# Gate and up of the four FFNs as seven block products over feature pairs, input halves and token halves

## The reference

```python
def rms_norm(x, g):
    y = x * lax.rsqrt(jnp.mean(x * x, axis=-1, keepdims=True) + RMS_EPS)
    return y * g
def swiglu(x, w_gate, w_up, w_down):
    return (jax.nn.silu(x @ w_gate) * (x @ w_up)) @ w_down
for layer in range(DEPTH):
    x = x + 0.5 * swiglu(rms_norm(x, ffn_norm1[layer]), ...)   # ffn0, ffn2
    h = rms_norm(x, mix_norm[layer])
    x = x + mixer(h)                      # mla_mixer, or swa with shared k, v
    x = x + 0.5 * swiglu(rms_norm(x, ffn_norm2[layer]), ...)   # ffn1, ffn3
    if layer == 0:
        kv = rms_norm(x, kv_norm) @ w_kv_shared
y = rms_norm(x, final_norm)
```

## Time and profile before

| | |
|---|---|
| median of 3 runs | 2532.2 us (2528.36 to 2532.36) |
| profiled execution | 2525.54 us, its span 2523.7 us |
| TensorE busy | 2455.3 us (97%), 16448 matmuls |
| VectorE, ScalarE, GpSimd busy | 46%, 30%, 35% |
| granted TensorE clock | 0.995 of full speed |
| HBM traffic | 83 GB/s over the span |

### The profile page before, as it was taken

One profiled execution on the slowest core, in us unless ns is written; L12 is line 12 of the kernel. 1 busy time (PEld: TensorE's weight loads), 2 busy tenths in 40 slices (PEclk: granted clock), 3 DMA queues, 4 the chain that ended last, 5 costly groups with the idle time before them and its releaser, 6 DMA issues.

```text
span 2523.7 us, 42391 instructions
## 1 busy us (share of the span) xinstructions
PE 2455.3 (97%) x16448; PEld 2340.2 (93%) x16448; DVE 1155.6 (46%) x2378; ACT 767.8 (30%) x1505; POOL 881.4 (35%) x592
## 2 busy tenths in 40 slices
PE   8999999998999999999999999999999999999997
PEld 8999999987666999999999999999986899999997
DVE  6434343665355453434346434343455464343435
ACT  6121222423255332121215222222246432222223
POOL 2333333443123334242424433333245243333332
PEclk9999999999999999999999999999999999999998
DMA  5222223234242122222222321212123122222211
GB/s 171 76 75 75 75 75 91 94 137 158 80 149 82 59 76 83 67 79 70 77 73 76 93 91 58 91 58 90 52 105 104 40 93 76 75 75 75 75 50 42
DMA packets 72607, 210.80 MB, mean 84 GB/s; under 512 B 7681, under 2 KB 22049, under 8 KB 71745
## 3 DMA queue, kind: packets, MB, share of 16 engines
q1 hardware_dynamic: 72512, 209.55, 26.3%
HBM read 191.22 MB, written 18.30 MB: 83 GB/s over the span
## 4 chain that ended last, share of the span: by engine, by line
PE 88%; DVE 4%; issue 2%; ACT 2%; POOL 1%; SPq 1%; DMA 1%; DVEq 0%; ACTq 0%; POOLq 0%
PE psa L356 17%; PE psa L357 17%; PE psa L358 17%; PE psb L356 10%; PE psb L357 10%; PE psb L358 10%; DVE split L479 1%; PE psb L1032 1%; PE psa L1168 1%; PE psa L1001 1%; PE psb L1187 1%; DVE work L404 1%; PE psb L1175 1%; PE psa L1002 1%; POOL wa L343 1%
## 5 line engine op out<-in xcount | busy, mean ns | idle before, releaser
L356 PE MATMUL psa<-split,wa 128*128 128x320 f32 (+1 forms) x3040 | 944.5, 311 | 24.4 <-DVE split L479 16.8
L358 PE MATMUL psa<-split,wa 128*128 128x320 f32 x3024 | 935.8, 309 | 0.0
L357 PE MATMUL psa<-split,wa 128*128 128x320 f32 x3024 | 935.7, 309 | 0.0
L343 POOL TENSOR_TENSOR wb<-raw,wb 128x1024 fp32r<-128x1024 f32 (+1 forms) x99 | 235.4, 2378 | 1205.6 <-ACT wb L335 1178.4
L356 PEld LDWEIGHTS psa<-split,wa 128*128 128x128 f32 x3040 | 573.9, 189 | 28.5 <-DVE wa L461 9.6
L357 PEld LDWEIGHTS psa<-split,wa 128*128 128x128 f32 x3024 | 570.8, 189 | 0.9 <-issue 0.2
L358 PEld LDWEIGHTS psa<-split,wa 128*128 128x128 f32 x3024 | 570.5, 189 | 0.0
L343 POOL TENSOR_TENSOR wa<-raw,wa 128x1024 fp32r<-128x1024 f32 x205 | 490.4, 2412 | 169.8 <-ACT wa L335 169.8
L356 PE MATMUL psb<-acts,wb 128*128 128x320 f32 x1440 | 447.4, 311 | 1.9 <-DVE xs L687 1.7
L687 DVE SCALAR_TENSOR_TENSOR xs<-psb,xs 128x320 f32<-128x320 f32 x720 | 341.3, 488 | 229.6 <-PE psb L358 229.6
L357 PE MATMUL psb<-acts,wb 128*128 128x320 f32 x1440 | 444.7, 309 | 0.0
(11 more groups left out here) (222 smaller groups left out, 2169.7 us busy)
## 6 DMA issues: line engine op xcount, KB each, us to landing
raw<-in_w SPq DMA_DIRECT2D x310, 512.0 KB, 3.9
park<-xs SPq DMA_DIRECT2D x2, 2560.0 KB, 9.0
work<-in_c_latT SPq DMA_DIRECT2D x8, 512.0 KB, 3.9
work<-in_c_lat SPq DMA_DIRECT2D x8, 512.0 KB, 3.6
xs<-park SPq DMA_DIRECT2D x1, 2560.0 KB, 14.5
xs<-park SPq DMA_DIRECT2D x2, 1280.0 KB, 5.5
y_out<-xs SPq DMA_DIRECT2D x8, 320.0 KB, 3.4
work<-v_park SPq DMA_DIRECT2D x8, 256.0 KB, 3.0
```

Of the source, the lines that this page charges most:

```text
L343: nc.gpsimd.tensor_tensor(lo[:, 0:n], raw[:, (p % RAW_SLOTS) * PIECE:(p % RAW_SLOTS) * PIECE + n], hi[:, 0:n].bitcast(F32), ALU.subtract). ...
L356: nc.tensor.matmul(ps, w[0], xx[1], start=first, stop=False)
L357: nc.tensor.matmul(ps, w[1], xx[0], start=False, stop=False)
L358: return nc.tensor.matmul(ps, w[0], xx[0], start=False, stop=last)
```

## The change

Two neighbouring feature tiles, the two halves of the 8 input tiles and the two token halves make a 2 x 2 by 2 x 2 block product, done with seven products in place of eight, for gate and for up. Of a pair's weights, VectorE forms the sums s1, s2, s3 and s4 in `raw` (`sum_first`, `sum_second`, `sum_fourth`), each operand of 128 x 512 is copied by ScalarE (`operand_hi`) and split by GpSimd (`operand_lo`) into a ring of 7 slots; there are 14 operands a pair (7 kinds, gate and up). The activations are now scaled with gain and `rstd` ahead of the first product (`x_first` for b11 and b21, `x_second` for t1, b22, t2, n4, t3), summed and split into seven parts that stay in place for the whole FFN; three of them lie in buffers of other phases, so the keys and values are stored and read back ahead of the window phase. Running sums in PSUM are copied out by ScalarE between products (`act_snap`), and VectorE adds a snapshot and a bank for three of the four (tile, half) results (`dve_combine`). Silu, product and its split are as before, and so are the down products, their order and their evictions. The transitions into the FFNs are rewritten: FFN1's squares and sums, which VectorE and ScalarE made ahead of it, are now made during the output projection, and the first weight sums and splits stand there too. The table of the window's biases is read behind FFN2.

The diff, cut to the loops of an FFN:

```diff
+KINDS = ("a11", "a12", "s1", "s2", "s3", "a22", "s4")
+X_OF = {"a11": "b11", "a12": "b21", "s1": "t1", "s2": "t2", "s3": "t3", "a22": "n4", "s4": "b22"}
+OPS = 2 * len(KINDS)
+GU = OPS * PAIRS
+SNAPS, SUMS, COMBS, PRODS = 6 * PAIRS, 8 * PAIRS, 3 * PAIRS, 4 * PAIRS
+RING, RING_AT = 7, 4
+QUARTER = DT // 2
+HALVES = {"a11": (0, 0), "a12": (0, 1), "s2": (0, 0), "s1": (1, 0), "a22": (1, 1), "s4": (0, 1)}
+SUM_TURN = {"s3": 0, "s1": 1, "s2": 4, "s4": 6}
+REGION = [dict(zip(("b11", "b21", "b22", "t2", "t1", "t3", "n4"), range(7)))] * 4
+REGION[2] = dict(zip(("n4", "b11", "b21", "b22", "t2", "t1", "t3"), range(7)))
...
+            place = ffn_place(p - RAW_SLOTS)
+            if place and place[2] < 4:
+                i, pair, n = place
+                sp.wait_ge(s_lo, at(it, 28, GU * i + OPS * pair + 13 + n // 2))
+            else:
+                sp.wait_ge(w_lo, at(it, 4, N_SINGLE[p - RAW_SLOTS + 1]))
...
+    def operand_hi(act, i, it, pair, j):
+        kind, m, n = KINDS[j // 2], j % 2, OPS * pair + j
+        if kind in ("a11", "a12", "a22"):
+            wait_landed(act, i, pair, m, HALVES[kind][0], it)
+        else:
+            act.wait_ge(s_sum, at(it, 16, SUMS * i + 8 * pair + SUM_TURN[kind] + (m if kind in ("s2", "s4") else 2 * m) + 1))
+        if n >= RING:
+            act.wait_ge(gu_mm, at(it, 28, GU * i + n - RING + 1))
+        elif i:
+            act.wait_ge(*RING_BEFORE[i][0 if (j + RING_AT) % RING >= 4 else 1])
+        nc.scalar.activation(ring_hi[:, (j + RING_AT) % RING, :], operand(i, pair, kind, m), ACT.Copy).then_inc(s_hi, 1)
...
+    def operand_lo(pool, i, it, pair, j):
+        r = (j + RING_AT) % RING
+        pool.wait_ge(s_hi, at(it, 28, GU * i + OPS * pair + j + 1))
+        nc.gpsimd.tensor_tensor(ring_lo[:, r, :], operand(i, pair, KINDS[j // 2], j % 2), ring_hi[:, r, :].bitcast(F32),
+                                ALU.subtract).then_inc(s_lo, 1)
...
+    def sum_first(dve, i, it, pair, m, kind):
+        if kind == "s3":
+            for f in range(2):
+                wait_landed(dve, i, pair, m, f, it)
+            if pair:
+                dve.wait_ge(s_lo, at(it, 28, GU * i + OPS * (pair - 1) + 8 + m + 1))
+            elif i:
+                dve.wait_ge(*RING_BEFORE[i][0])
+            nc.vector.tensor_tensor(s3_of[m], raw_half(i, pair, m, 0, 0), raw_half(i, pair, m, 1, 0), ALU.subtract).then_inc(s_sum, 1)
+        else:
+            nc.vector.tensor_tensor(raw_half(i, pair, m, 1, 0), raw_half(i, pair, m, 1, 0), raw_half(i, pair, m, 1, 1), ALU.add).then_inc(s_sum, 1)
+    def sum_second(dve, i, it, pair, m):
+        dve.wait_ge(s_lo, at(it, 28, GU * i + OPS * pair + m + 1))
+        dve.wait_ge(s_sum, at(it, 16, SUMS * i + 8 * pair + 2 * m + 2))
+        nc.vector.tensor_tensor(raw_half(i, pair, m, 0, 0), raw_half(i, pair, m, 1, 0), raw_half(i, pair, m, 0, 0), ALU.subtract).then_inc(s_sum, 1)
+    def sum_fourth(dve, i, it, pair, m):
+        dve.wait_ge(s_lo, at(it, 28, GU * i + OPS * pair + 2 + m + 1))
+        dve.wait_ge(s_sum, at(it, 16, SUMS * i + 8 * pair + 4 + m + 1))
+        nc.vector.tensor_tensor(raw_half(i, pair, m, 0, 1), raw_half(i, pair, m, 0, 1), raw_half(i, pair, m, 0, 0), ALU.subtract).then_inc(s_sum, 1)
...
+    def x_hi(act, i, kind):
+        hi, lo = x_parts[REGION[i][kind]]
+        for k in range(QUARTER):
+            src = {"b11": tmp11, "b21": tmp21, "t1": tmp12, "t2": x_full[REGION[i]["t3"]]}.get(kind)
+            act.wait_ge(x_val, 32 * i + VALUE[kind] + k + 1)
+            nc.scalar.activation(hi[:, k, :], (x_full[REGION[i][kind]] if src is None else src)[:, k, :], ACT.Copy).then_inc(x_hid, 1)
+    def x_lo(dve, i, kind, k):
+        hi, lo = x_parts[REGION[i][kind]]
+        src = {"b11": tmp11, "b21": tmp21, "t1": tmp12, "t2": x_full[REGION[i]["t3"]]}.get(kind)
+        dve.wait_ge(x_hid, 28 * i + SPLIT[kind] + k + 1)
+        nc.vector.tensor_tensor(lo[:, k, :], (x_full[REGION[i][kind]] if src is None else src)[:, k, :], hi[:, k, :].bitcast(F32),
+                                ALU.subtract).then_inc(x_split, 1)
+    def x_scaled(dve, i, out, d, h):
+        s = N_FFN[i]
+        nc.vector.scalar_tensor_tensor(out=out, in0=x[:, d, half(h)], scalar=consts[:, DT * s + d:DT * s + d + 1],
+                                       in1=rstd[:, half(h)], op0=ALU.mult, op1=ALU.mult).then_inc(x_val, 1)
+    def x_first(dve, i, kind):
+        dve.wait_ge(n_rstd, 2 * SUM_OF[N_FFN[i]] + 1)
+        tmp, d0 = (tmp11, 0) if kind == "b11" else (tmp21, QUARTER)
+        for k in range(QUARTER):
+            x_scaled(dve, i, tmp[:, k, :], d0 + k, 0)
+            if k:
+                x_lo(dve, i, kind, k - 1)
+        x_lo(dve, i, kind, QUARTER - 1)
+    def x_second(dve, i, free, weights):
+        dve.wait_ge(n_rstd, 2 * SUM_OF[N_FFN[i]] + 2)
+        done = lambda kind, k: dve.wait_ge(x_val, 32 * i + VALUE[kind] + k + 1)
+        b22, t2, n4 = (x_full[REGION[i][r]] for r in ("b22", "t3", "n4"))
+        for k in range(QUARTER):
+            x_scaled(dve, i, tmp12[:, k, :], k, 1)
+        for s, v in free:
+            dve.wait_ge(s, v)
+        for k in range(QUARTER):
+            done("b12", k)
+            nc.vector.tensor_tensor(tmp12[:, k, :], tmp12[:, k, :], tmp11[:, k, :], ALU.subtract).then_inc(x_val, 1)
+        for k in range(QUARTER):
+            x_scaled(dve, i, b22[:, k, :], QUARTER + k, 1)
+            x_lo(dve, i, "t1", k)
+        for k in range(QUARTER):
+            done("b22", k)
+            nc.vector.tensor_tensor(t2[:, k, :], b22[:, k, :], tmp12[:, k, :], ALU.subtract).then_inc(x_val, 1)
+            if k:
+                x_lo(dve, i, "t2", k - 1)
+        x_lo(dve, i, "t2", QUARTER - 1)
+        weights()
+        if i == 2:
+            dve.wait_ge(stored, 32)
+        done("t2", QUARTER - 1)
+        for k in range(QUARTER):
+            nc.vector.tensor_tensor(n4[:, k, :], tmp21[:, k, :], t2[:, k, :], ALU.subtract).then_inc(x_val, 1)
+        for k in range(QUARTER):
+            nc.vector.tensor_tensor(t2[:, k, :], t2[:, k, :], tmp11[:, k, :], ALU.subtract).then_inc(x_val, 1)
+        for kind in ("t3", "n4", "b22"):
+            for k in range(QUARTER):
+                x_lo(dve, i, kind, k)
...
+    def pe_gate_up(pe, i, it, pair, entry=None):
+        for j in range(OPS):
+            kind, m, r = KINDS[j // 2], j % 2, (j + RING_AT) % RING
+            combined = gate_out if m == 0 else up_out
+            pe.wait_ge(s_lo, at(it, 28, GU * i + OPS * pair + j + 1))
+            if kind == "a11":
+                bank = psa[:, 2 * m, 0:HT]
+                if pair:
+                    pe.wait_ge(prod_done if m else silu_done, at(it, 8, PRODS * i + 4 * pair - 1))
+                else:
+                    for s, v in entry:
+                        pe.wait_ge(s, v)
+            elif kind == "a12":
+                bank = psb[:, m, 0:HT]
+                if pair:
+                    pe.wait_ge(combined, at(it, 6, COMBS * i + 3 * pair - 2))
+                    pe.wait_ge(x_upd, at(it, 32, OUT_BASE[f"ffn{i}"] + N_OUT * (pair - 2) + 13 + m))
+                elif i:
                     pe.wait_ge(x_upd, OUT_BASE[f"ffn{i}"])
+            elif kind == "s1":
+                bank = psa[:, 2 * m + 1, 0:HT]
+                if pair:
+                    pe.wait_ge(combined, at(it, 6, COMBS * i + 3 * pair))
+            elif kind == "s4":
+                bank = psa[:, 2 * m + 1, 0:HT]
+                pe.wait_ge(combined, at(it, 6, COMBS * i + 3 * pair + 2))
+            else:
+                bank = psa[:, 2 * m, 0:HT]
+                pe.wait_ge(snapped, at(it, 12, SNAPS * i + 6 * pair + {"s2": 0, "s3": 2, "a22": 4}[kind] + m + 1))
+            fresh = kind in ("a11", "a12", "s1")
+            hi, lo = x_parts[REGION[i][X_OF[kind]]]
+            for k in range(QUARTER):
+                if it is None and pair == 0:
+                    pe.wait_ge(x_split, 28 * i + SPLIT[X_OF[kind]] + k + 1)
+                last = mm3(bank, (ring_hi[:, r, lot(k, P)], ring_lo[:, r, lot(k, P)]), (hi[:, k, :], lo[:, k, :]),
+                           fresh and k == 0, k == QUARTER - 1, not fresh)
+            last.then_inc(gu_mm, 1)
+            if it is None and pair == 0 and j == 0 and i != 2:
+                pe_norm_sum(pe, N_FFN[i], 1)
+            if it is None and pair == 0 and j == 5 and i == 0:
+                pe_bias(pe)
...
+        pe_gate_up(pe, i, None, 0, entry)
         with pe.Fori(0, FFN_LOOPS) as it:
             for cc in range(2):
+                pe_gate_up(pe, i, it, 1 + cc)
                 pe_down(pe, i, it, cc)
+        pe_down(pe, i, None, PAIRS - 1)
...
+    def act_first(act, i):
+        o = lambda j: operand_hi(act, i, None, 0, j)
+        x_hi(act, i, "t1")
+        act_snap(act, i, None, 0, 0)
+        o(7)
+        act_snap(act, i, None, 0, 1)
+        x_hi(act, i, "t2")
+        o(8)
+        o(9)
+        o(10)
+        x_hi(act, i, "t3")
+        o(11)
+        x_hi(act, i, "n4")
+        o(12)
```

(124 more changed lines are left out.)

554 lines of the change are left out of this document (269 added, 285 removed).

## The result

The changed kernel takes 2573.3 us (median of four runs, 2572.4 to 2585.2) against 2532.3: ratio 1.017, interval 1.014 to 1.021. It is slower by 41 us, and 39 above the forecast of 2534. The profiled execution took 2573.5 us with a span of 2571.7, which is 48.0 more than the span before.

A forecast was written before the change was run, and what follows sets the result against it. TensorE, busy 97% of the span, was taken to bound the kernel. Fewer matmuls -126.6, steady-pair waits +68 and FFN entries +60 gave +2 us: 2534 us, own range 2505 to 2562, whole range 2475 to 2590.

The forecast's parts named there:

- rival (b): In each down, VectorE busy without a gap bounds it through GpSimd port meetings: 3 us a pair, 2579 us, chance 0.17.
- the sum's +2 us: Whole kernel: -126.6 for fewer matmuls, +68 for steady-pair waits, +60 for FFN entries, on the profiled execution's 2525.5 us.
- entries well off 10, 12, 11 and 27: At FFN starts, delays far from 10 (FFN2), 12 (FFN1), 11 (FFN3), 27 us (FFN0) would show the forecast wrong.
- Matmuls gone: Gate and up products: 168 instead of 192 matmuls a pair, count down by 1056, saving 126.6 us behind the first downs.
- Steady chain: Through four engines, a late load of the next pair's operand delays TensorE's fifth down group by 1.2 us.
- the working: Timetable of engine starts and durations for a steady pair and the FFN entries, giving 1.9 us a pair and +60.
- The port meeting: In each pair, VectorE's low part of product 2 meets GpSimd's split of the next operand 1: 1.15 us a meeting.
- the second term, the meetings further on in the down: Later in each down, VectorE's two-operand instructions meet GpSimd's splits: 0.5 or 0.9 us, within 1.9 a pair.
- The Trainium skill's rule: VectorE with two SBUF inputs and GpSimd exclude each other for whole instructions: 1.3 instead of 1.15 us, some 5 overall.
- Entries: Before each FFN's first down, preparing activations delays TensorE: 10, 12, 11 and 27 us, together +60, bounds 45 and 80.
- Clock: At the FFN entries, waits might lower TensorE's granted clock: taken as nothing, bounds 0 and 8 us.
- (a): In steady downs, the four-engine chain arrives in time: 0.5 us a pair, 2478 us, chance 0.27.

The follow-up runs named there:

- The experiments on the order and on the port: Changed kernel each: ScalarE's entry order changed, 2575.8 us; VectorE's, 2564.4; GpSimd's pair 0 low parts cut to 64 of 512 columns in FFN1 to FFN3, 2556.8.
- The first experiment: Changed kernel with ScalarE's copy of the next pair's operand 1 moved behind the copy of product 2 and silu 3: 2512.8 us.

## Where the prediction was right and where wrong, point by point

2573.3 us lies outside the forecast's own range (2505 to 2562) and inside the whole one (2475 to 2590) only because that took in rival (b), whose mechanism is not what the runs show. Against the sum's +2 us the profile has +48: 21 less in the steady pairs, 41 more at the entries, 21.5 at the first downs, which the sum lacked, and 4.4 elsewhere. Two errors of opposite sign partly cancelled, which was luck. The sign of being wrong that the prediction named, entries well off 10, 12, 11 and 27, came: 21.7, 20.5, 25.2 and 33.8.

- **Matmuls gone**: right, 1056, and 38.7 us a pair once nothing waits.
- **Steady chain**: right in every link. From snapshot 5 the working had `o(1)`'s copy at +7.8, VectorE's low part done at +10.2 and the fifth group at +11.5 us; the trace has 7.9, 10.2 and 11.5. The port meeting took 1.33 us instead of 0.49. The fifth group is late by 1.2 us, as in the working, and with its slower first matmul that is all of the 1.32. Mis-sized was the second term, the meetings further on in the down: nothing is lost there where the working had 0.7. +48 instead of +68. The Trainium skill's rule ("SBUF — State Buffer", section "Who interferes with whom"), was weighed against the change. Its second half, that one SBUF input doesn't contend, holds here too: `dve_out`, with one PSUM and one SBUF input, took 479 ns in the mean of 720 and never over 494, beside GpSimd's splits or not.
- **Entries**: the term that failed, 101 instead of 60. The step is where VectorE's second half of x begins. The working had it at 1.8 us in FFN2, as if the first half were prepared under the projection; it came at 10.4, behind scaled products, low parts and two weight sums (3.27 us) in the same queue. That is 9 us late; the lateness is 5 us in FFN1 (start 22.1, working 17.1), 13 in FFN3 (15.0, working 2.2) and 2 in FFN0: 29 of the 41. This is read from the timelines; no run starts the second half earlier with everything else as it was. From that start on the working held in FFN2: t2 after 13.7 us (working 14.7), product 8 after 24.8 (25.9). The rest, 1 to 5 us in each FFN, lies behind product 8, where two products run at half clock and ScalarE loads a table (1.28 us). The experiments on the order and on the port show that what sets this stretch is VectorE's work beside GpSimd.
- **Missing term**: the first down of each FFN. I ended the entry at its start and took the steady pair from there. But pair 0's chain has no lead, and its lateness comes out in that down: +21.5. The first experiment, which moves one line, takes 16.7 of it away together with the steady wait.
- **Clock**: taken as 0, bounds 0 to 8; filled waits gave 5.5. Inside the bounds, and the reason given holds: where VectorE sets the pace, a half clock costs little. The clock was 0.67 from 1450 to 1460 us behind a wait of 3.63, and 1.00 with the wait filled. That waits lower it is also what the Trainium skill says ("TensorE: Matmul & The Clock Gate", part 1).
- **Rivals**: (b)'s time, 2579, is near the result, its mechanism isn't: VectorE waits 3.93 us in each down, and a gap-free down was its condition. (a), the chain in time, is not this kernel but is one line from it.

So the gain of 126.6 us is there in full, since TensorE did bound the kernel; against it stand 48 for a new wait per pair, 101 for the entries and 21.5 for the first downs.

## What to carry to other kernels

Where one in-order queue holds both a copy that waits for a load and the copy that the critical engine needs, put the load's copy last; here a timetable from row durations found such a knot to 0.1 us. Fewer matmuls paid for by more work on the vector engines cost nothing in the steady state, once the queues were in the right order, and most of the gain where a stage begins without a lead: there count the whole queue of the busiest engine from its first instruction, what stands ahead included. When a wait of TensorE is attacked, say first which engine has no idle time behind it; here, where its work didn't shrink, the wait mostly moved.

## What the runs showed of the hardware

The granted clock cost time elsewhere than it was looked for. One stretch of attention, 600 to 640 us, which no edit touches, has a clock of 0.96 in the changed kernel and 0.83 in others; with the same stalls at 610 to 625 us the clock fell either for a moment or for some 15 us of matmul work:
```profile
600.00:640.00 40.00, 34.88 (x187) 27.12 (x186) 23.02 (x49) 11.76 (x29) 15.93 (x15) 0.96 0.46 164
```
```profile
600.00:640.00 40.00, 33.56 (x157) 24.93 (x156) 20.97 (x45) 9.24 (x23) 14.92 (x13) 0.83 0.46 163
```
(changed kernel, then the one with filled waits). FFN1's first scaled product comes 9.6 us later in the second, though the two stood within 0.1 us of each other at 600 us, and 6.4 of the 9.6 are there at 642 us; this hides what the fill gained. From FFN0's last down to that product the profiled executions take 385 us in the one kernel with a clock of 1.00 in this stretch, 388 to 390 in the six with 0.91 to 0.98, and 395 to 398 in the four with 0.83. Five runs of the kernel with half of d0's split had mean clocks of 0.974, 0.971, 0.969, 0.968 and 0.965 and spans of 2542.6, 2546.6, 2552.1, 2550.5 and 2557.3 us: in one program the clock alone goes with 15 us. What decides between the two is not shown by these runs.
